# Expert weights loaded as pairs in 2 MB transfers, and 32 rows for the smallest expert, in a two-layer decoder trunk

## The reference, cut to what matters

```python
top_val, top_idx = lax.top_k(logits, TOP_K)          # 2 of 8 experts for each of 256 tokens
hb = jax.nn.silu(xb @ w1[e]) * (xb @ w3[e])          # w1, w3: 1024 x 3584 f32
return hb @ w2[e]                                    # w2: 3584 x 1024 f32
```

## Time and profile before

| | us |
|---|---|
| median of the three timed runs | 1381.05 |
| profiled execution, first to last instruction (span) | 1379.9 |
| PE busy / DVE busy / ACT busy in the span | 1356.7 / 905.6 / 672.8 |
| DMA: 500.56 MB, 72862 packets, mean | 363 GB/s |
| expert stage, first matmul to end of the last unit | 546.8 to 1365.5 |

### The profile page before, as it was taken

How to read it: one execution, slowest core, us unless ns; L and a number is a source line. 1 busy time by engine, 2 the same in 40 slices (tenths; PEclk the granted TensorE clock), 3 DMA queues, 4 the chain that set the end, 5 groups by cost and what they waited for, 6 DMA issues and landing times.

```text
span 1379.9 us, 18423 instructions
## 1 busy us (share of the span) xinstructions
PE 1356.7 (98%) x7372; PEld 1025.3 (74%) x7372; DVE 905.6 (66%) x1103; ACT 672.8 (49%) x773; POOL 54.3 (4%) x125
## 2 busy tenths in 40 slices
PE   9999999999999999999999999999999999999995
PEld 6788879878788888567777677777677777777752
DVE  6899979978778964116575674656575666668513
ACT  2784463533467444026365544554563655546311
POOL 6000000000000000100000000000000000000020
PEclk9999999999999999999999999999999999999998
DMA  9929939988554679899999999999999999999995
GB/s 371 418 91 363 392 120 402 412 319 347 203 208 153 245 299 403 360 419 421 421 421 412 421 421 421 420 404 422 421 419 409 420 394 414 423 421 421 421 420 217
DMA packets 72862, 500.56 MB, mean 363 GB/s; under 512 B 8512, under 2 KB 8640, under 8 KB 15298
## 3 DMA queue, kind: packets, MB, share of 16 engines
q1 hardware_dynamic: 69986, 490.91, 87.5%
q0 software_dynamic: 2784, 8.41, 1.7%
HBM read 496.12 MB, written 4.21 MB: 363 GB/s over the span
## 4 chain that ended last, share of the span: by engine, by line
PE 92%; DVE 5%; DMA 2%; ACT 1%; issue 1%; DVEq 0%; POOL 0%; ACTq 0%; POOLq 0%
PE ps L2094 21%; PE ps L2608 20%; PE ps L2096 20%; PE ps L2095 20%; PE ps L2156 2%; PE ps L2588 2%; PE ps L2649 2%; DMA raw<-in_moe_w_dram 2%; DVE lo L1378 1%; DVE raw L1319 0%; DVE mx L1612 0%; DVE r L1620 0%; ACT hi L843 0%; PE ps L2304 0%; DVE r L1610 0%
## 5 line engine op out<-in xcount | busy, mean ns | idle before, releaser
L1406 DVE TENSOR_TENSOR lo<-raw,hi 128x2048 fp32r<-128x2048 f32 x138 | 311.4, 2287 | 86.6 <-ACT hi L860 86.5
L2094 PE MATMUL ps<-hi,hT_hi 128*128 128x512 f32 (+3 forms) x912 | 355.1, 389 | 3.6 <-DVE hT_lo L1432 1.9
L2096 PE MATMUL ps<-hi,hT_lo 128*128 128x512 f32 (+3 forms) x912 | 348.9, 383 | 0.0
L2095 PE MATMUL ps<-lo,hT_hi 128*128 128x512 f32 (+2 forms) x844 | 322.1, 382 | 0.0
L860 ACT ACTIVATE hi<-raw 128x2048 fp32r<-128x2048 f32 x138 | 257.3, 1915 | 4.8 <-DMA raw<-in_moe_w_dram 4.8
L2094 PEld LDWEIGHTS ps<-hi,hT_hi 128*128 128x128 f32 x912 | 171.2, 188 | 47.7 <-issue 13.5
L2096 PEld LDWEIGHTS ps<-hi,hT_lo 128*128 128x128 f32 x912 | 171.2, 188 | 32.6
L1378 DVE TENSOR_TENSOR lo<-raw,hi 128x2048 fp32r<-128x2048 f32 (+3 forms) x82 | 174.7, 2143 | 24.8 <-ACT hi L843 23.5
L2095 PEld LDWEIGHTS ps<-lo,hT_hi 128*128 128x128 f32 x844 | 158.6, 188 | 27.5
L2094 PE MATMUL ps<-hi,bT_hi 128*128 128x512 f32 (+2 forms) x416 | 163.9, 394 | 0.4 <-DVE bT_lo L1626 0.4
L2608 PE MATMUL ps<-raw,bT_first 128*64 128x256 f32 (+1 forms) x1048 | 159.3, 452 | 4.4 <-DMA raw<-in_moe_w_dram 4.4
(11 more groups left out here) (367 smaller groups left out, 1252.0 us busy)
## 6 DMA issues: line engine op xcount, KB each, us to landing
raw<-in_moe_w_dram SPq DMA_DIRECT2D x275, 1024.0 KB, 9.7
r<-in_moe_w_dram SPq DMA_DIRECT2D x52, 1024.0 KB, 9.8
raw<-in_w_ada_dram SPq DMA_DIRECT2D x40, 1024.0 KB, 7.6
raw<-in_w_fd_dram SPq DMA_DIRECT2D x11, 1024.0 KB, 8.7
raw<-in_w_ga_dram SPq DMA_DIRECT2D x8, 1024.0 KB, 8.0
raw<-in_w_gb_dram SPq DMA_DIRECT2D x8, 1024.0 KB, 6.8
raw<-in_w_ab_dram SPq DMA_DIRECT2D x8, 1024.0 KB, 7.2
raw<-in_w_fg_dram SPq DMA_DIRECT2D x8, 1024.0 KB, 8.6
```

Of the source, the lines that this page charges most:

```text
L1406: dve.tensor_tensor(low_of(r), raw_of(r), high_of(s).bitcast(f32), ALU.subtract).then_inc(raw_done, 1)
L2094: pe.matmul(o, wh, mh, start=first, stop=False)
L2095: pe.matmul(o, wh, ml, start=False, stop=False)
L2096: return pe.matmul(o, wl, mh, start=False, stop=last)
```

## The change

Four things are done. (1) The host lays each step's weights out as 128 rows of 16 KB (`lay_out`). From chunk 26 on the places are used in six fixed pairs whose members lie side by side (`ROW_OF`, `PAIRS`), and one DMA fills a pair with 2 MB; both readers wait for the same semaphore, and the next DMA into a pair waits until both its chunks are used. The last two chunks (334, 335) stay single. (2) `RETURN` goes from 27 to 26, so chunk 26 no longer takes a place in `hi`. (3) The expert with the fewest tokens (item 7, `TINY`) gets 32 rows: `beside` puts four matmuls side by side, each over a quarter of the weight's columns; its scatter writes quarter rows. (4) Item 7 changes places with item 6: its units are now 26, 29, 31, 34, 36, 39 and 42, and the last units belong to item 6, with 64 rows as before.

```diff
-RETURN = 27
+RETURN = 26
+PAIRED = 26
+LAST_PAIR = EXPERTS * PER_ITEM - 2
+ROW_OF = (1, 6, 3, 8, 4, 0, 7, 2, 5)
+PAIRS = ((5, 0), (7, 2), (4, 8), (1, 6), (3, NRAW), (NRAW + 1, NRAW + 2))
...
+    for c in range(PAIRED, ITEMS * PER_ITEM, 2):
+        pairs = sorted(p for p in pairs if not (p[1] > NRAW and c >= LEAVE or p[2] == NRAW and c >= EXPERTS * PER_ITEM))
+        _, a, b = pairs.pop(0)
+        pairs.append((NR + c + 1 + HELD, a, b))
...
-SMALL_ITEMS = (0,) + tuple(range(LARGE, EXPERTS))
+TINY = EXPERTS - 1
+TINY_CAP = P // 4
+SMALL_ITEMS = (0, 5, TINY, 6)
...
-END = EXPERTS - 1
+END = SMALL_ITEMS[-1]
...
-PREPS = (0, 1, 5, 2, 6, 3, 7, 4)
+PREPS = (0, 1, 5, 2, 7, 3, 6, 4)
...
+def small_cap(i):
+    return TINY_CAP if i == TINY else HALF_CAP
+def up_width(n):
+    return GRP * small_cap(UNITS[n][0]) // P
...
-                sp.dma_start(raw_of(r), src).then_inc(raw_full[RING[r][0]], 16)
+                if paired(c):
+                    sp.wait_ge(used, NW + max(RING[NR + c + half][2] for half in range(2)) - NR + 1)
+                    sp.dma_start(pair_of(NR + c), src).then_inc(raw_full[RING[NR + c][3]], 16)
+                    return
+                for half in range(2):
+                    r = NR + c + half
+                    slot_free(r)
+                    sp.dma_start(raw_of(r), src[:, half * CH:(half + 1) * CH]).then_inc(raw_full[RING[r][3]], 16)
...
+            pool.tensor_scalar(above[:, :], tok_i[:, 0:1], P - TINY_CAP - 0.5, None, ALU.is_gt)
+            link(pool.tensor_scalar(row_quarter[:, :], tok_i[:, 0:1], TINY_CAP - 0.5, None, ALU.is_gt))
+            link(pool.tensor_tensor(row_quarter[:, :], row_quarter[:, :], upper[:, :], ALU.add))
+            link(pool.tensor_tensor(row_quarter[:, :], row_quarter[:, :], above[:, :], ALU.add))
...
+            for q in range(P // TINY_CAP):
+                pool.tensor_copy(slots_t[:, q * TINY_CAP:(q + 1) * TINY_CAP], slots[:, 0:TINY_CAP]).then_inc(tiny_slots, 1)
...
+                dve.tensor_scalar(ov, order, TINY - 0.5, float(HALF_CAP - TINY_CAP), ALU.is_gt, ALU.mult)
                 link(dve.tensor_scalar(capx, order, LARGE - 0.5, float(HALF_CAP), ALU.is_lt, ALU.mult))
+                link(dve.tensor_tensor(capx, capx, ov, ALU.subtract))
...
-            def beside(bank, width, stationary, w, at, first, last):
-                for q in range(2):
-                    m = pe.matmul(ps[q * HALF_CAP:(q + 1) * HALF_CAP, bank, 0:width], stationary,
+            def beside(bank, total, cap, stationary, w, at, first, last):
+                width = total * cap // P
+                for q in range(P // cap):
+                    m = pe.matmul(ps[q * cap:(q + 1) * cap, bank, 0:width], stationary,
                                   w[:, at + q * width:at + (q + 1) * width], start=first, stop=last)
...
-                for c in range(2 if SMALL[n] else 4):
+                for c in range(up_width(n) // P if SMALL[n] else 4):
                     m = pe.transpose(ps[:, 2, c * P:(c + 1) * P], src[:, c * P:(c + 1) * P], ident[:, :])
...
-        w[0].reshape(EXPERTS, 2, 4, P, NG, GRP).transpose(0, 4, 1, 3, 2, 5)).reshape(EXPERTS, NG, 2, P, CH)
+        w[0].reshape(EXPERTS, 2, 4, P, NG, GRP).transpose(0, 4, 3, 1, 2, 5)).reshape(EXPERTS, NG, P, 2 * CH)
...
-        "moe_w2": rows_of(i["moe_w2"][0], 2).reshape(EXPERTS, NG, 2, P, CH),
+        "moe_w2": rows_of(i["moe_w2"][0], 4).reshape(EXPERTS, NG, P, 2 * CH),
```

More of the change, by code:

```diff
@@ L167, in raw_ring, with fill @@
     out, free, fills, last = [], [(0, slot) for slot in range(NRAW)], [0] * PLACES, [None] * PLACES
-    for r in range(NR + ITEMS * PER_ITEM):
+    def fill(slot, r, by):
+        out.append((slot, fills[by], last[slot], by))
+        last[slot] = r
+    for r in range(NR + PAIRED):
         c = r - NR
@@ L173, in raw_ring @@
         _, slot = free.pop(0)
[L174 to L175 removed]
+        while slot >= HIGH_AT and c >= RETURN:
             _, slot = free.pop(0)
@@ L178, in raw_ring, with paired @@
         fills[slot] += 1
-        out.append((slot, fills[slot], last[slot]))
-        last[slot] = r
+        fill(slot, r, slot)
+    at = {slot: n for n, slot in free}
+    pairs = [(max(at[a], at[b]), a, b) for a, b in PAIRS]
+    for c in range(PAIRED, ITEMS * PER_ITEM, 2):
+        pairs = sorted(p for p in pairs if not (p[1] > NRAW and c >= LEAVE or p[2] == NRAW and c >= EXPERTS * PER_ITEM))
+        _, a, b = pairs.pop(0)
+        pairs.append((NR + c + 1 + HELD, a, b))
+        fills[a] += 1
+        if c == LAST_PAIR:
+            fills[b] += 1
+        fill(a, NR + c, a)
+        fill(b, NR + c + 1, b if c == LAST_PAIR else a)
     return out
 RING = raw_ring()
-LAST_IN = [max(r for r, (s, _, _) in enumerate(RING) if s == slot) for slot in range(PLACES)]
+LAST_IN = [max(r for r, place in enumerate(RING) if place[0] == slot) for slot in range(PLACES)]
+def paired(c):
+    return c >= PAIRED and c != LAST_PAIR
 GATES = [(l, v) for l, v in ADA if v in (G_M, G_F)]
@@ L203, in item_order @@
     for g in range(NG):
[L204 removed]
+        out += [(spot(kind, g, 0), kind, g) for kind in ("w1", "w3")]
         if g:
[L206 removed]
+            out.append((spot("w2", g - 1, 0), "w2", g - 1))
     return out
[L210 removed]
+LAST = [(PER_ITEM - 2, "w2", NG - 1)]
 DRAIN = (7, 0, 1, 2)
@@ L627, in unit_loads @@
                     i, g = UNITS[n]
-                    for half in range(2):
-                        moe_load(NR + unit_chunk(n, kind, half), kind, expert[i], g, half)
+                    moe_load(unit_chunk(n, kind, 0), kind, expert[i], g)
             def item_loads(i, e):
-                for c, kind, g, half in item_order() + LAST:
-                    moe_load(NR + i * PER_ITEM + c, kind, e, g, half)
+                for c, kind, g in item_order() + LAST:
+                    moe_load(i * PER_ITEM + c, kind, e, g)
             for n, (i, g) in enumerate(UNITS):
```

87 lines of the change are left out of this document (54 added, 33 removed).

## The result

The changed kernel takes 1374.17 us, median of four runs (1373.68 to 1374.42), against 1381.24 us for the kernel before (four runs, 1380.88 to 1383.16): ratio 0.9946, 95% interval 0.9935 to 0.9958, 7.1 us faster. Its profiled execution took 1374.42 us, with a span of 1372.7.

A forecast was written before the change was run, and what follows sets the result against it. DMA and TensorE both looked full, so the smaller of two gains counts: DMA 5.2 + 3.8 - 2.5 = 6.5 us against TensorE's 11.4. Span 1379.9 - 6.5 = 1373.4, plus 1.15, gives 1374.5 us; range 1366 to 1384.

The forecast's parts named there:

- What bounds: Whole kernel: DMA and TensorE within 2% of each other, DMA ending last by 4.4 us; the smaller gain counts.
- TensorE's sum: TensorE's total gain: 7 us from seven tiny-expert units plus 4.4 us of end waits, 11.4 us.
- the term of w1 and w3: Tiny-expert units: 64 instructions each at 59 ns take 3.80 us, capped near 3.50; a unit goes from 10.49 to 9.50.
- the 4.4 us of waits at the end: Last four halves of w2: TensorE's waits for weights, counted as 4.4 us of TensorE's gain.
- DMA, rows: Weight transfers: 72 packets fewer a chunk at 6.3 ns save 28 ns; over 182 chunks, 5.2 us.
- DMA, idle time recovered: From 940 us on: TensorE's saving lifts the DMA from 417 to 421 GB/s over 400 us, 3.8 us.
- The pair at the end: End of kernel: a pair's first half waits until both chunks land, a cost of 2.5 us.
- From span to time: Forecast span of 1373.4 us to run time: profiled span lies 1.15 us under the runs' median, giving 1374.5 us.
- Edits at nothing: POOL setup and copies, VectorE's small instructions, scatter, fewer DMA issues, lost lead at the start: all costed at nothing.
- Rows don't pay: Rival, DMA packets: no fixed packet cost, or 16 KB moves as two packets; 1.3 us gained, 1379.8 us, chance 0.18.
- Two side by side: Rival, tiny expert on TensorE: quarters run in twos, only end waits of 4.4 us gained; 1376.7 us, chance 0.07.
- issue sets the pace: Rival, tiny expert's 160 instructions: issue spacing sets unit time, slower above 69.5 ns; 1392.8 at 80, 1428.6 at 112; chance 0.15.

The follow-up runs named there:

- tiny_only: Changed kernel with single 1 MB chunks and 8 KB rows as before the change, keeping 32 rows for the tiny expert: 1378.95 us, ratio 0.9980.
- pairs_only: Changed kernel with 64 rows for all small experts, keeping 16 KB rows and pairs: 1380.38 us, ratio 0.9990.
- pad36: Changed kernel with 36 transposes of 128 columns added to each of the tiny expert's 7 units: 1375.62 us, ratio 0.9951.
- by_quarter: Changed kernel with the tiny expert's w1 and w3 matmuls reordered, four in a row on one quarter of the array before the next: 1378.56 us, ratio 0.9980.
- pairs_8k: Changed kernel with the same 2 MB transfers into pairs, but laid out in rows of 8 KB instead of 16 KB: 1383.29 us, ratio 1.0011.
- singles_end: Changed kernel with the last 8 chunks single instead of the last 2: 1374.02 us, ratio 0.9952.
- pairs_from_150: Changed kernel with single chunks (8 KB rows) up to chunk 149 and pairs only from chunk 150 on: 1375.15 us, ratio 0.9958.
- late_gathers: Changed kernel with POOL's four gathers of the experts' rows held until the last unit's w1 is used: 1372.67 us, ratio 0.9938.
- tiny_early_gathers: Changed kernel with the tiny expert second instead of third in the small set, and gathers held until the last unit's w1 is used: 1371.28 us, ratio 0.9931.

## Why the prediction was right

**What bounds.** That DMA and TensorE are within 2% of each other, and that the kernel gets the smaller of two gains, held: `tiny_only` and `pairs_only` each gave less than half of what both give.

**TensorE's sum: the term of w1 and w3 was mis-sized.** 3.80 us for 64 instructions, at 59 ns from the line L2320 in the earlier trace rows; measured 1.89 us, 29.5 ns. The prediction took that row as a pace at which instructions follow one another. In the trace's records it is two halves of the array at work: the instructions start in twos, 7 ns apart, and the twos some 109 ns apart. Beside the 112 ns of the full width in the earlier trace rows it already said one, two, and so perhaps four at once; 29.5 is half of 59. A unit gave 5.0 us instead of 1.0, the sum 35 + 4.4 us instead of 11.4. It hardly reached the time, since TensorE's sum was the larger one either way; `pad36`, with a unit at the predicted 9.5 us, is 1.4 us slower (0.7 by the ratios).

**TensorE's sum: the 4.4 us of waits at the end didn't belong in it.** They are waits for a full DMA, and the changed kernel still has 1.91 + 0.93 + 1.44 = 4.3 us of them. `pairs_only`, in which TensorE gives nothing but these waits, gained 1.3 us. So "it doesn't matter how much more than 2.1 us TensorE gives" was too low a bar: `by_quarter`, with 0.2 us a unit or 1.3 us in all, stays 4.4 us above the changed kernel. With the 35 us that four quarters gave, neither error reached the time.

The Trainium skill ("TensorE: Matmul & The Clock Gate", Back-to-back issue gap) has about 81 ns a matmul for a sustained stream with 128 columns; no run here is bound by such a pace, not even `by_quarter` with 67.

**DMA, rows.** 28 ns a chunk were taken; 421 to 427 GB/s is 2.491 - 2.456 us = 35 ns. And it isn't 72 packets at 6.3 ns, but 64 data packets at 8.7 ns; the 8 tiny ones cost nothing that shows (`pairs_8k`). The Trainium skill ("DMA: Bandwidth & Descriptors", Why small descriptors are slow) has 3 cycles a packet, from which the prediction's estimate was 0.6% for 8 against 16 KB; the stretches show 1.4% (427 against 421 GB/s). The 176.3 MB that move from 940 us to the last landing are 168 chunks' worth: 5.9 us for the predicted 5.2.

**DMA, idle time recovered.** 3.8 us, and it happened: the DMA is full from 940 to 1340 us. Alone (`tiny_only`) it gave 2.8.

**The pair at the end: this term failed.** "The first half of a pair can be used only when both have landed" is true, and TensorE does wait for pairs (1.91 us before 1342.78), but the waits don't move the last landing, which is set by the DMA's queue: `singles_end` gained nothing of the 2.5 us. In their place something else of about that size was missing from the sum: the changed kernel is behind in bytes at 940 us, 323.17 MB against 324.05, 0.9 MB or 2.1 us. 0.5 MB of them arise from 540 us on: 560:600 loses (378 - 326) x 40 us = 2.1 MB; 540:560, 600:640 and 640:940 bring back 0.3, 0.2 and 1.0 MB. The other 0.4 MB are missing before 540 us already, before the first pair is issued, and no run says whether they come of the change. Nor is it shown whether the first part comes of the places or of the step to pairs (see `pairs_from_150`). 5.9 + 3.8 - 2.1 = 7.6 us against 7.2 measured at the last landing; 0.4 us aren't explained. So the total of 6.5 was near 7.1 in part by luck: a term that wasn't there stood for one of its size that was left out.

**From span to time.** The prediction added 1.15 us, one execution's span against the median of others. Each execution here takes 1.7 us more than its own span (1374.42 against 1372.7), so the same sum would give 1375.1; that error of 0.6 us was on the lucky side too.

**Edits at nothing** held as far as it shows: no wait for weights stands near 620 us, and PE is busy 40 of 40 us in 600:640. What POOL's and VectorE's new instructions cost, no run isolates.

**The rivals.** "Rows don't pay" falls by the rate, and `pairs_8k` shows what it would have been: not 1379.8, but 1383.3. "Two side by side" and "issue sets the pace" fall by the 29.5 ns; `pairs_only` shows what the first would have been: not 1376.7, but 1380.4. `by_quarter` shows that the order of the matmuls decides how many quarters are at work.

## What to carry to other kernels

Where two resources are within 2%, price a change on both and run each half alone: the halves gave 1.3 and 2.8 us, the pair 7.1. Put the relief of the slower resource where the other one first has something to gain: the same tiny expert some 260 us earlier (first unit at 660 instead of 918 us) gave 2 to 3 us more for a change of order. And where a full DMA sets the end, as here, waits of the engines before the last landing had no price (`singles_end`), but bytes queued ahead of the last chunk have one, the 2 MB of gathers among them, until the gathers themselves come last (`late_gathers`, `tiny_early_gathers`).

## What the runs showed of the hardware

**Four quarters.** f32 instructions with 32 stationary columns and 128 moving ones start 109 ns apart on one quarter of the array. What changes is how many quarters are at work: four if neighbouring matmuls stand on different quarters (64 instructions in 1.89 us, 29.5 ns each), and no more than two in runs of four matmuls on one quarter (4.3 us, 67 ns each, `by_quarter`).

**The clock after a wait.** TensorE of the changed kernel in order of time around its first long wait, then the granted clock there (column before the last two):

```profile
992.90 0.77 PE L2160 MATMUL ps<-hi,bT_hi 128*128 128x512 f32 x1 [5.53 <-DVE bT_lo L1982]
...
994.32 0.63 PE L2160 MATMUL ps<-hi,bT_hi 128*128 128x512 f32 x1
...
999.24 0.39 PE L2160 MATMUL ps<-hi,bT_hi 128*128 128x512 f32 x1
999.46 0.39 PE L2161 MATMUL ps<-lo,bT_hi 128*128 128x512 f32 x1
...
986.00:993.00 7.00, 1.47 (x53) 1.23 (x44) 3.09 (x3) 4.44 (x5) 0.00 (x0) 0.94 1.01 426
993.00:999.00 6.00, 6.00 (x14) 4.67 (x15) 5.89 (x8) 4.83 (x3) 2.22 (x1) 0.50 1.01 431
999.00:1005.00 6.00, 6.00 (x28) 4.97 (x27) 5.89 (x3) 2.54 (x2) 0.00 (x0) 1.00 1.01 428
```

After a wait of 5.5 us the granted clock is 0.50, the lower of the two levels, 1.2 GHz: matmuls of 512 columns start 0.42 us apart instead of 0.22, for 6 us. That costs about 3 us of TensorE's time for each such wait. There are three of them in 940:1340 (5.53, 5.41 and 5.18 us; a fourth of 1.63 us leaves the clock at 1.00), which is why the mean there is 0.97. The DMA was full all the while (426 to 431 GB/s), so the time doesn't show it, and in `pad36`, where TensorE has work instead of waits, it doesn't occur (1.00).

**A late chunk costs more than its lateness.** A large unit's w2 waits for a chunk, its high part on ScalarE (1.9 us) and its low part on VectorE (2.3 us), and VectorE does the unit's own hidden rows (L1982, 0.6 us) only behind that split, as the lines below show. So the wait that the trace books on `bT_lo` (17.7 us in four pieces) is one for weights. The chain there:

```profile
969.94 18.00 DMA raw<-in_moe_w_dram
...
987.97 1.92 ACT hi L915
...
989.91 2.29 DVE lo L1465
992.20 0.61 DVE bT_lo L1982
```
